# Five gathered rows instead of six per ring, four scaled rows instead of two, in a hybrid attention and expert-retrieval layer

## The reference

```
h = layer_norm(x)
p = h @ w_in + b_in            # q latent, kv latent, rotary key, Fourier channels, two sets of gate logits
y_a = latent attention         # 8 heads, 96-wide q and k (64 + 32 rotary), 1024 x 1024 scores, dense
y_f = real part of a 2-D DFT over positions and 128 channels, 4 groups, then a linear map
m = sigmoid(g0) * y_a + sigmoid(g1) * y_f
h = layer_norm(alpha * h + m @ w_out + b_out)
```

```
q = h @ w_q                                  # per token 8 heads x 2 halves of 128
s_half = q . keys                            # 128 scores per half
top 16 of each half, 16 x 16 sums, top 16    # 16 experts per head, 128 per token
gate = softmax(top scores)
a[t, e] = gelu(x[t] . w_u[expert]) * gate    # w_u row, 1024 wide
y[t]    = sum_e a[t, e] * w_v[expert]        # w_v row, 1024 wide
out = layer_norm(alpha * h + y)
```

## Time and profile before

| | |
|---|---|
| median of 3 runs | 3676.09 us |
| lowest, highest | 3662.14, 3679.78 us |
| the profiled execution's own time | 3666.81 us |
| its span, from first to last instruction | 3665.0 us |
| TensorE busy | 2779.8 us (76%) |
| GpSimd busy | 2356.0 us (64%) |
| VectorE busy | 2220.9 us (61%) |
| ScalarE busy | 1612.2 us (44%) |
| DMA moved | 1240.83 MB, mean 339 GB/s |
| of it the gathers | 1073.87 MB |

### The profile page before, as it was taken

One profiled execution on the slowest core, in us unless ns is written; L12 is line 12 of the kernel. 1 busy time (PEld: TensorE's weight loads), 2 busy tenths in 40 slices (PEclk: granted clock), 3 DMA queues, 4 the chain that ended last, 5 costly groups with the idle time before them and its releaser, 6 DMA issues.

```text
span 3665.0 us, 40824 instructions
## 1 busy us (share of the span) xinstructions
PE 2779.8 (76%) x14008; PEld 2205.7 (60%) x14008; DVE 2220.9 (61%) x5004; ACT 1612.2 (44%) x1842; POOL 2356.0 (64%) x2075
## 2 busy tenths in 40 slices
PE   6999986667788776677788776678787776666676
PEld 3456855556676565556675665567775665555555
DVE  5044148547865578457765686477765785466643
ACT  1121013445554555455554554455454454444444
POOL 3000007766677777766778787666777777777775
PEclk9999997578799898587899896687899985655556
DMA  4224539999999999999999999999999999999998
GB/s 170 92 92 144 172 125 341 384 344 327 330 399 409 409 409 386 376 340 317 360 409 409 409 393 376 374 338 328 373 409 409 409 382 373 408 364 357 359 396 344
DMA packets 350432, 1240.83 MB, mean 339 GB/s; under 512 B 38480, under 2 KB 46160, under 8 KB 349712
## 3 DMA queue, kind: packets, MB, share of 16 engines
q0 software_dynamic: 294912, 1073.87, 76.7%
q1 hardware_dynamic: 34096, 117.94, 8.8%
q10 hardware_dynamic: 21216, 46.40, 3.6%
HBM read 1222.33 MB, written 15.73 MB: 338 GB/s over the span
## 4 chain that ended last, share of the span: by engine, by line
POOL 29%; PE 24%; DMA 18%; issue 11%; DVE 8%; ACT 5%; DVEq 3%; SPq 0%; ACTq 0%; POOLq 0%
DMA rows<-in_peer_v,ids_peer 17%; POOL rows L310 15%; POOL rows L319 15%; PE acc L600 5%; ACT av L1099 4%; PE fA L483 3%; PE m L567 2%; PE fA L523 2%; PE m L371 2%; DVE small L760 2%; PE acc L589 1%; PE fB L341 1%; DVE rows L872 1%; PE m L467 1%; PE m L499 1%
## 5 line engine op out<-in xcount | busy, mean ns | idle before, releaser
L600 PE MATMUL acc<-ident,av 128*128 128x128 f32 x8192 | 1471.9, 340 | 762.1 <-ACT av L1099 747.5
L600 PEld LDWEIGHTS acc<-ident,av 128*128 128x128 f32 x8192 | 1212.0, 176 | 1036.0 <-ACT av L1099 965.1
L310 POOL DMA_INDIRECT rows<-in_peer_u,ids_peer x1024 | 1151.3, 1124 | 828.2 <-DVE ids_peer L852 348.9
L872 DVE CUSTOM_DVE_ANT_0 rows<-rows,hh 128x1024 f32<-128x1024 f32 x1024 | 1241.9, 1222 | 698.1 <-DMA rows<-in_peer_u,ids_peer 687.2
L1099 ACT ACTIVATE av<-rows,coef 128x1024 f32<-128x1024 f32 x1024 | 1164.2, 1145 | 1107.8 <-DMA rows<-in_peer_v,ids_peer 1001.6
L319 POOL DMA_INDIRECT rows<-in_peer_v,ids_peer x1024 | 1156.7, 1130 | 318.9 <-issue 278.1
L567 PE MATMUL m<-hT_g,wring 128*128 128x256 f32 x1024 | 254.3, 406 | 1.1 <-ACT hT_g L1061 1.1
L523 PE MATMUL fA<-hT_g,wring 128*128 128x256 f32 x1024 | 233.7, 383 | 0.0
L567 PEld LDWEIGHTS m<-hT_g,wring 128*128 128x128 f32 x1024 | 206.9, 208 | 31.2 <-ACT hT_g L1061 1.5
L523 PEld LDWEIGHTS fA<-hT_g,wring 128*128 128x128 f32 x1024 | 193.3, 193 | 24.9
L1030 ACT ACTIVATE S<-fA,small 128x1024 f32<-128x1024 f32 x64 | 71.3, 1114 | 266.1 <-DVE small L762 266.1
(11 more groups left out here) (153 smaller groups left out, 2183.2 us busy)
## 6 DMA issues: line engine op xcount, KB each, us to landing
wring<-in_wstream SPq DMA_DIRECT2D x192, 512.0 KB
ln<-in_dft_seq ACTq DMA_DIRECT2D x32, 512.0 KB, 3.5
rows<-in_peer_u,ids_peer POOLq DMA_INDIRECT x1024, 7.1
rows<-in_peer_v,ids_peer POOLq DMA_INDIRECT x1024, 7.1
hT_g<-in_x SPq DMA_DIRECT2D x8, 512.0 KB, 3.6
hres_spill<-KT ACTq DMA_DIRECT2D x8, 512.0 KB, 2.7
hT_spill<-rows ACTq DMA_DIRECT2D x1, 4096.0 KB, 11.1
wring<-in_wstream SPq DMA_DIRECT2D x16, 256.0 KB
```

The source lines that it names most:

```text
L310: pool.indirect_dma_start(u_rows[:, ring(g, i, NU), :], None, peer_u, bass.IndirectOffsetOnAxis(ap=ids_peer[:, t, s:s + 1], axis=0)).then_ ...
L600: last = mm(acc[:, tok(k)], av[:, i % NAV, tok(k)], ident[:, :], is_transpose=True, start=i % SLOTS == 0 and k % 4 == 0, stop=i % SLOTS == ...
L872: v.tensor_tensor_reduce(out=row, in0=row, in1=h1_peer[:, t, :], scale=1.0, scalar=0.0, op0=ALU.mult, op1=ALU.add, accum_out=dots[:, b, i ...
```

## The change

The rings of gathered u rows and of gathered v rows go from six to five rows each, and the ring of scaled rows from two to four. The on-chip memory of the three together stays 14 rows.

```
-NU = NV = 6
-NAV = 2
+NU = NV = 5
+NAV = 4
```

## The result

| | before | with the change |
|---|---|---|
| median of 8 runs | 3677.81 us | 3697.76 us |
| lowest, highest | 3662.14, 3692.88 us | 3686.89, 3704.96 us |
| profiled execution, its own time | 3666.81 us | 3697.90 us |

The ratio is 1.0056, 95% interval 1.0032 to 1.0080: slower by 20 us. The eight runs before include the three on which the forecast stood. I had forecast 3685 us in a range of 3655 to 3745.

A forecast was written before the change was run, and what follows sets the result against it. Compute was taken to bound attention and the DMA the weight stretch. Terms 1.5 + 11.8 = 13.3 us gave 3680.1 us on the profiled execution, 3689.4 on the median; the middle, 3685 us, was forecast, range 3655 to 3745.

The forecast's parts named there:

- Steady attention: Steps 10 to 60 of three groups, bound by a compute chain: 0.5 us lost per group where VectorE is held up, 1.5 us.
- the signs that I had named: In attention GpSimd's wait for dots grows from 28.9 us per 160 us while the slot stays at 3.33 us.
- 8.2 us in a cycle of 16.7: Attention: issue, landing and dot need 8.2 us of the 16.7 us that five slots of 3.33 us give a row.
- One slot of lead at each change to the weight stretch: Attention to weight stretch: one slot of 3.11 us lost in three groups, plus 2.53 us in the last, sum 11.8 us.
- the last group's tile end: Step 64 of the last group, where VectorE finishes a tile: one lean slot lost, 2.53 us.
- Weight stretch: Steps 80 to 191, weights streamed beside gathers: fewer gathers in flight, landing falls to about 11 us, GB/s stays, 0 us.
- Rival A: The weight stretch loses its full DMA because landing stays at 14.1 us: 64 us slower there, 3744 us in all, chance 0.17.
- Lean stretches: Gathers alone, as in the last group's tail: GpSimd waits for no dot, so five rows are as good as six, 0 us.
- Scaled rows: Four scaled rows: ScalarE's waits for TensorE, 66.4 us, are followed by later waits, so they give 0 us.
- the bound that I set: Whole kernel: within 0.5% of 3676 us, 18.4 us, counts as no change.
- signs of being wrong: Weight stretch under 400 GB/s or landing over 13 us, attention slots below 3.25 us, row waits mid-attention, lean slot time moving.
- rival B: Four scaled rows pay, as ScalarE no longer waits for TensorE: up to 66.4 us gained, 3614 us, chance 0.13.

The follow-up runs named there:

- experiment 1: Five u, five v and two scaled rows against the kernel before (six, six, two), the shortened rings alone: 3693.39 us, ratio 1.0053.

## Why the prediction was right, and where not

1. *Steady attention, 1.5 us.* Not settled. Steps 0 to 60 of the three groups took 605.1 us in both profiled executions, by gather v's starts. But the granted clock of TensorE differed; these steps in the second group, before and with the change:

```profile
1547.40:1747.00 199.60, 151.97 (x874) 126.37 (x872) 135.88 (x282) 102.68 (x117) 131.00 (x121) 0.80 0.93 332
...
1552.50:1752.20 199.70, 144.41 (x885) 118.66 (x886) 139.86 (x287) 105.49 (x121) 133.73 (x121) 0.86 0.92 335
```

The same time at a clock of 0.86 instead of 0.80 can hide a loss. In the other comparisons the same steps took 6.1 us more with five rows and two scaled rows, 13.2 more with five u and six v rows, 12.7 more with gather v first and 5.1 more in the pair of runs without the dot's second input; with six u and five v rows 0.7 less. These are single executions at clocks that differ again, and groups of one kernel differ by 5 us (205.0, 199.6 and 200.5 before), so a loss here of 0 to 13 us is possible and none is shown. Against the signs that I had named, GpSimd did not wait longer for dots (21.8 against 28.9 us), and ScalarE waited for v rows (12.7 us); the latter came with the four scaled rows, as experiment 1 shows, and not from rows that landed later. With four rows the same steps lose 25.4 us. The margin there is thinner than 8.2 us in a cycle of 16.7 made it look; that this is because VectorE's dots come in bunches is my reading and was not tested.
2. *One slot of lead at each change to the weight stretch, 11.8 us.* This is the main term and it held: 8.7 us in steps 60 to 96 of the three groups against 9.3, and in four other comparisons 7.9 to 11.6. For the last group's tile end I had 2.5; steps 60 to 88 there took 3.7 us more, together 12.4 us. In the pair of runs without the dot's second input these steps took only 0.7 us more.
3. *Weight stretch, 0 us.* Right: 409 GB/s, landing 11.3 us as forecast, and even eight rows (four and four) gave 404 GB/s. Rival A, which would have cost 64 us, did not come.
4. *Lean stretches, 0 us.* In the profiled execution wrong: the tail had 380 instead of 409 GB/s in its window, and its slot 2.74 instead of 2.53 us. The prediction had weighed longer gathers and said that they come only where GpSimd waits for dots anyway and has slack. In this tail GpSimd waits for no dot, and the gathers that start behind a running dot take up to 1.93 us, the second pace; it comes and goes at either depth, and the pair without it showed 0.4 us there.
5. *Scaled rows, 0 us.* Right as far as 0.3% tells: with and without them 1.0056 and 1.0053. The 47.4 us by which ScalarE's wait for TensorE shrank were off the path, as the earlier trace rows had said.

The sum was 13.3 us against 20 measured (12 to 29 by the interval, 13.8 in the pair of runs without the dot's second input). The 3685 us were only 9 us above the median then known, since I had taken the middle between two bases; the sum on that median is 3689 us. By the bound that I set, the measured 0.56% lies a little past no change, on the side to which I had given 0.37; I had given 0.50 to no change. What is left of the difference, some 7 us, is within the interval and was not traced to a place; attention is one where it could lie.

Three of the signs that I had called signs of being wrong appeared: ScalarE waiting for v rows in attention, a lean stretch whose slot time moved, and an attention slot below 3.25 us (2 x 160/100 = 3.20 by the count of the window, which is off since it holds other steps; over steps 0 to 60 the slot is as before). Yet neither rival A nor rival B came. A sign read from a fixed window of time, or from one execution, is weaker than one read between the same steps of several versions.

Which ring: the prediction said that both are held back by the u ring. The one-at-a-time runs agree (1.0014 for v, 1.0072 for u), and so does the table.

## What to carry to other kernels

Ask of each ring which stretch uses it up. In this kernel a row less cost nothing where transfers are the bound and enough are still in flight (rate times landing), and about one slot at every change from a compute-bound to a transfer-bound stretch, because that is the lead that had been stored. Where several rings feed one engine that issues in order, look for the ring that closes first: here shortening the other cost nothing measurable, and lengthening the first alone moved the wait to the other. To find such a loss, count between the same steps where a slot is used, and in several versions; where it is issued, the lead and the pace are mixed. A wait that a deeper buffer removes is worth nothing if the same engine waits next for something later.

## What was not expected of the hardware

- A gather instruction on GpSimd takes 0.94 us alone and up to 2.2 us when it starts behind a running VectorE instruction with two SBUF inputs; one that starts before the dot keeps its 0.94 us. Replacing this one VectorE instruction by one with a single input took 359 us off GpSimd's busy time and 84 us off the kernel.
- Five gathers of 512 KB in flight fill the DMA (409 GB/s at 6.6 us landing in the lean tail). More only lengthen the landing: in the lean tail of the kernel with one input, 81 gathers in 100 us at 12.3 us landing are ten in flight, at the same 409 GB/s. In the weight stretch, beside the weights' chunks, it was 11.3 us at seven and 14 us at nine, at 409 GB/s too.
- One chip of those used ran the same kernel in 3863 us instead of 3672.
